# Modulation work ahead of the attention steps, gate rows by a product with ones, and one product less before the first unit

## Chip, cores and metric

One core of a Trainium2 chip runs the whole kernel; its time is the device time of one launch in microseconds (us). Engines are named as the profile names them: PE (TensorE matmul) and PEld (its weight load), DVE (VectorE), ACT (ScalarE), POOL (GpSimd), SP (SyncE, which here only starts transfers). Clock figures are the granted clock of PE, 1.00 being 2.4 GHz and 0.50 being 1.2 GHz.

## The reference

Two transformer blocks on one sequence of 256 tokens, width 2048, all in float32. What matters here is the first block's modulation: twelve thousand numbers computed from a condition vector c, in six parts of 2048 (shift, scale and gate of the two half-blocks).

```python
c_act = jax.nn.silu(c)
mod = c_act @ w_ada[l] + b_ada[l]                  # w_ada: 2048 x 12288
sh1, sc1, gt1, sh2, sc2, gt2 = [m[:, None, :] for m in jnp.split(mod, 6, axis=-1)]
h = rms_norm(x, g_norm1[l]) * (1 + sc1) + sh1
proj = h @ w_in[l]
...                                                # differential and latent attention, 8 heads each
mix = jnp.concatenate([a_out, b_out], axis=-1) @ w_out[l]
x = x + gt1 * mix
h2 = rms_norm(x, g_norm2[l]) * (1 + sc2) + sh2
ffn = (jax.nn.silu(h2 @ w_gate[l]) * (h2 @ w_up[l])) @ w_down[l]
x = x + gt2 * ffn
```

The second block (convolution and attention branches, a feed-forward of 8192) follows and is not touched.

## The kernel before

**Units.** All large products are made of units (`unit`, L620 on PE). A unit multiplies 256 rows of a weight matrix by 512 columns: 12 matmuls of 512 columns, since each float32 product is made as three products of float32r halves (high by high, high by low, low by high). A weight load is 1 MB and feeds two units. SP issues all loads in one fixed order (`ORDER`) into a ring of four buffers (`raw`); a load waits until the one four places before it is used up. Before a unit can run, ACT writes the high half of its weights (`split`, L1154), then DVE the low half (L1678). Each engine's program has one slot per unit: in its slot ACT and DVE make a split three units ahead, then do what hangs on that unit.

**Modulation.** w_ada comes in 96 loads `a`. The first 32 (`NPRO`) go through a ring of their own of four buffers (`early_mix`, `wide`), the rest through `raw`, between the weight loads. For loads 0 to 79 PE multiplies by the condition columns (`part_sums`, L643: four matmuls side by side, each with 32 output rows; 512 columns), and DVE copies or adds the bank into the tile `part` (L1724, L1729, L1731). When a group is complete, `part_columns` (L670) brings it to one number per partition: four small products with `sel` or `ones` (L677, L680), to which DVE adds the bias (L1747, L1759) in `mcol`. Loads 80 to 95 (gate gt2) are multiplied on DVE instead (`part_products`, L1697), inside the first loop of the feed-forward. The two gates gt1 and gt2 are needed as rows, the same in all partitions: `part_row` (L684, L690) multiplies each column of `mcol`, broadcast, by the identity, four matmuls of 128 columns for 512 numbers, and DVE copies the bank to `grow` (L1767), a tile that shares memory with `v_tok`.

**Where it is placed.** `prologue` (L110) lists the steps before the first unit: products 0 to 17, the turning of x (`normT`), the gains. `modulation(u)` (L127) lists the modulation steps of unit u: until unit 15 one product per unit, then a pair of products in each of 24 units between 24 and 98, with `columns` steps between them; gt1's groups are complete in units 88 and 100, and `gt1_row` makes its four rows behind units 93, 97, 101 and 105. gt2's groups get a column product in one unit of the loop and the row product in the next.

**Order within a slot.** On PE a unit's 12 matmuls come first, then `run(todo)`, the attention steps of this unit as listed by `window` and `heads_at`, and then `modulate()`:

```python
                last_mm.then_inc(unit_used, 1)
                run(todo)
                modulate()
```

DVE's slot has the same order: split, attention steps, modulation. ACT takes no part in the modulation but counts the banks. The small products of both kinds go through two PSUM banks in turn (`wait_bank`, L607): a step has to wait until the step two places before it has been read out, whoever reads it. Attention steps are, among others, `qbT`, `kvbT` (transposes, L716), `da` and `ha` (head products, L829, L855), `dc` (L838), with their DVE parts `qbN` (L2007), `kvbN` (L2031, L2034), `daW` and so on.

**First units.** ACT's order before the first unit is split 0, split 1, `modulated(0)` (L1273, scales the first chunks of x), split 2, `modulated(1)` and on; DVE's is column sums of the scale, split 0, split 1, its half of `modulated(0)` (L1931, L1932, which releases `h_ready`), split 2, `modulated(1)`.

## Time and profile before

| | us |
|---|---|
| median of 3 runs | 2669.9 (2666.29 to 2670.49) |
| profiled execution, its time | 2669.09 |
| its span in the profile | 2667.0 |
| PE busy | 2594.2 (97%) |
| DVE busy | 1547.3 (58%) |
| ACT busy | 1164.6 (44%) |
| PE's granted clock, mean | 0.989 |

The profiled execution's time is 0.8 us below the median of the runs and 2.1 us above its own span. PE is busy nearly all the time; the page's slices show lower values only in the first (6 tenths) and in those from 267 us to 600 us (down to 8 tenths). The transfers' share is 0.9 in the first two slices and 0.5 to 0.7 behind them. "Idle before" names, in brackets behind an instruction, how long its engine waited and who released it.

### The profile page before, as it was taken

How to read it: one execution, taken by the hardware profiler on the slowest of the kernel's cores; microseconds unless marked ns; L12 is line 12 of the kernel's file. 1: busy time of each engine (PE TensorE's matmuls, PEld its weight loads, DVE VectorE, ACT ScalarE, POOL GpSimd, SP SyncE). 2: the span in 40 equal slices, each digit the busy share in tenths (PEclk: the TensorE clock that was granted, in tenths of full speed). 3: DMA queues.
4: the chain of work that ended last, by engine and by line, in shares of the span. 5: the costliest groups of instructions: out<-in, count | busy, mean ns of one | idle time of the engine just before them, and what ended most of it. 6: DMA issues, size and time to landing. Idle time of an engine off the chain costs nothing.

```text
span 2667.0 us, 32922 instructions
## 1 busy us (share of the span) xinstructions
PE 2594.2 (97%) x12142; PEld 2084.7 (78%) x12142; DVE 1547.3 (58%) x1700; ACT 1164.6 (44%) x1522; POOL 53.9 (2%) x86
## 2 busy tenths in 40 slices
PE   6999989899999999999999999999999999999997
PEld 2667757688888888887888888888888888888886
DVE  1456754567776555557655454556555555555555
ACT  2344554343434444443544455444444444444443
POOL 1010110000000000000000000000000000000000
PEclk8999989999999999999999999999999999999999
DMA  9967776657777655555655545566565555555652
GB/s 391 381 232 288 261 252 220 223 171 244 243 244 245 192 190 189 189 190 189 206 189 189 174 158 166 196 201 226 188 200 189 190 188 189 189 189 188 190 188 100
DMA packets 262881, 561.72 MB, mean 211 GB/s; under 512 B 9250, under 2 KB 13556, under 8 KB 261900
## 3 DMA queue, kind: packets, MB, share of 16 engines
q1 hardware_dynamic: 260688, 549.25, 61.2%
q0 software_dynamic: 1728, 9.19, 1.0%
q10 hardware_dynamic: 380, 2.13, 0.2%
q8 instruction: 56, 0.92, 0.1%
q14 instruction: 29, 0.24, 0.0%
HBM read 556.32 MB, written 4.21 MB: 210 GB/s over the span
## 4 chain that ended last, share of the span: by engine, by line
PE 83%; DVE 2%; ACT 1%; issue 1%; DMA 0%; POOL 0%; DVEq 0%; POOLq 0%; ACTq 0%
PE acc L633 78%; PE bank L716 2%; PE bank L663 1%; DVE w_lo L1678 0%; PE acc L857 0%; PE acc L909 0%; PE acc L855 0%; PE bank L728 0%; PE bank L866 0%; DMA raw<-in_w_ada 0%; PE bank L690 0%; DVE wide L2194 0%; DVE x_res L2198 0%; PE acc L1068 0%; PE acc L1069 0%
## 5 line engine op out<-in xcount | busy, mean ns | idle before, releaser
L1678 DVE TENSOR_TENSOR w_lo<-raw,w_hi 128x1024 fp32r<-128x1024 f32 x852 | 1037.7, 1224 | 827.5 <-ACT w_hi L1154 798.6
L1154 ACT ACTIVATE w_hi<-raw 128x1024 fp32r<-128x1024 f32 x852 | 901.0, 1060 | 1065.1 <-PE acc L633 953.8
L633 PE MATMUL acc<-w_hi,actT_hi 128*128 128x512 f32 (+1 forms) x2112 | 833.6, 395 | 1.2 <-DVE actT_lo L1813 0.8
L633 PE MATMUL acc<-w_hi,actT_lo 128*128 128x512 f32 (+1 forms) x2112 | 821.2, 389 | 0.0
L633 PE MATMUL acc<-w_lo,actT_hi 128*128 128x512 f32 (+1 forms) x2112 | 820.8, 389 | 0.0
L633 PE MATMUL acc<-w_hi,mixT_hi 128*128 128x512 f32 (+1 forms) x1280 | 504.3, 394 | 9.1 <-DVE mixT_lo L1803 4.3
L633 PE MATMUL acc<-w_hi,mixT_lo 128*128 128x512 f32 (+1 forms) x1280 | 498.0, 389 | 0.0
L633 PE MATMUL acc<-w_lo,mixT_hi 128*128 128x512 f32 (+1 forms) x1280 | 497.6, 389 | 0.0
L633 PEld LDWEIGHTS acc<-w_hi,actT_hi 128*128 128x128 f32 x2112 | 397.3, 188 | 106.5 <-issue 21.9
L633 PEld LDWEIGHTS acc<-w_hi,actT_lo 128*128 128x128 f32 x2112 | 397.1, 188 | 83.0
L633 PEld LDWEIGHTS acc<-w_lo,actT_hi 128*128 128x128 f32 x2112 | 397.7, 188 | 79.3 <-issue 1.2
L633 PEld LDWEIGHTS acc<-w_hi,mixT_hi 128*128 128x128 f32 x1280 | 241.1, 188 | 67.5 <-issue 9.4
L633 PEld LDWEIGHTS acc<-w_hi,mixT_lo 128*128 128x128 f32 x1280 | 240.9, 188 | 49.7
L633 PEld LDWEIGHTS acc<-w_lo,mixT_hi 128*128 128x128 f32 x1280 | 241.3, 189 | 47.5
L2171 DVE TENSOR_TENSOR x_res<-x_res,acc 128x1024 f32<-128x1024 f32 x68 | 83.0, 1221 | 30.4 <-PE acc L633 30.4
L663 PE MATMUL bank<-raw,ccol 128*32 128x512 f32 x384 | 48.8, 617 | 5.4 <-DMA raw<-in_w_ada 3.1
L716 PE MATMUL bank<-cst,work 128*128 128x128 f32 x356 | 47.9, 274 | 5.5 <-DVE att L2034 2.5
L716 PEld LDWEIGHTS bank<-cst,work 128*128 128x128 f32 x356 | 41.8, 141 | 13.9 <-DVE att L2034 2.9
L2171 DVE TENSOR_TENSOR wide<-wide,acc 128x1024 f32<-128x1024 f32 x36 | 44.0, 1221 | 14.5 <-PE acc L633 14.5
L1202 ACT ACTIVATE mixT_hi<-bank 128x512 fp32r<-128x512 f32 (+1 forms) x54 | 25.6, 503 | 60.6 <-PE bank L716 37.4
L1458 ACT ACTIVATE work<-acc,kpe 128x512 f32<-128x512 f32 x48 | 30.4, 686 | 39.3 <-PE acc L633 39.3
L1707 DVE SCALAR_TENSOR_TENSOR part<-raw,ccol,part 128x512 f32<-128x512 f32 x60 | 45.1, 751 | 1.7
(272 smaller groups left out, 1049.1 us busy)
## 6 DMA issues: line engine op xcount, KB each, us to landing
raw<-in_w_ff SPq DMA_DIRECT2D x128, 1024.0 KB, 5.1
raw<-in_w_in SPq DMA_DIRECT2D x108, 1024.0 KB, 5.2
raw<-in_w_ada SPq DMA_DIRECT2D x64, 1024.0 KB, 5.2
raw<-in_w_gate SPq DMA_DIRECT2D x44, 1024.0 KB, 5.1
raw<-in_w_up SPq DMA_DIRECT2D x44, 1024.0 KB, 5.2
raw<-in_w_down SPq DMA_DIRECT2D x44, 1024.0 KB, 5.1
early_mix<-in_w_ada SPq DMA_DIRECT2D x16, 1024.0 KB, 9.5
wide<-in_w_ada SPq DMA_DIRECT2D x16, 1024.0 KB, 8.8
```

The source lines that it names most:

```text
L633: last_mm = pe.matmul(acc[p][:, t, 0:width], act[x][:, k0 + c, t * P:(t + 1) * P], w[:, u % SPL, c * NW:c * NW + width], start=first and c ...
L663: ins = pe.matmul(dst[32 * j:32 * j + 32, :], ccol[:, 2 * r + j // 2 if n_ == 8 else 4 * r + j, :], src[:, j * NW:(j + 1) * NW], start=beg ...
L716: ins = pe.transpose(bank[b][:, j * P:(j + 1) * P], src_of(j), ident)
L1154: act.activation(w_hi[:, u % SPL, :], raw[:, ld % RAW, (u % DU) * 1024:(u % DU + 1) * 1024], ACT.Copy) \
L1202: act.activation(dst, bank[b][:, 0:n], ACT.Copy).then_inc(bank_hi, 1)
L1458: ins = act.activation(stg[:, t * NW:(t + 1) * NW], acc[p][:, t, :], ff, scale=scale[:, t:t + 1])
L1678: dve.tensor_tensor(w_lo[:, u % SPL, :], raw[:, ld % RAW, (u % DU) * 1024:(u % DU + 1) * 1024], w_hi[:, u % SPL, :].bitcast(F32), ALU.subt ...
L1707: ins = dve.scalar_tensor_tensor(out=part[:, :], in0=src, scalar=ccol[:, k, 0:1], in1=part[:, :], op0=ALU.mult, op1=ALU.add)
L2171: link(dve.tensor_tensor(dst[:, :, g * NW:(g + 1) * NW], dst[:, :, g * NW:(g + 1) * NW], acc[g % 2][:, :, :], ALU.add))
```

## The change

1. **Order in a slot.** On PE, DVE and in ACT's count of banks, the modulation steps of a unit come ahead of its attention steps.
2. **Gate rows.** The `columns` step of the six groups of gt1 and gt2 goes, and with it `gt1_row`. In its place `part_row` multiplies `part` itself: two matmuls of 512 columns with a broadcast column of `sel` for a group of gt1 (1024 numbers), two of 256 columns with `ones` for one of gt2 (512 numbers), each in a bank of its own. DVE no longer copies but adds the bank to `grow`, which holds the bias already: POOL loads it, spread over all partitions (1 MB), gt1's behind the last differential head, gt2's once x is updated. gt1's rows are now made in units 88 and 100. gt2's column and row steps are now one step, in the unit of the former column step.
3. **First unit.** Product 17 moves from the prologue into unit 0, behind its matmuls. On DVE split 0 comes ahead of the last `columns` step of the prologue, split 1 behind `modulated(0)`.
4. The bias rows of gt1 and gt2 are no longer loaded at the start (two small transfers of POOL less).

```diff
-    return steps + [("part", LEAD), ("part", LEAD + 1)]
+    return steps + [("part", LEAD)]
...
-        return [LEAD + 1 + v] if 0 < v < NPRO - LEAD - 1 else []
-    events = [("row", n) for a in products(u - 3) for n in completed(a) if n >= len(GROUPS)]
-    events += [("columns", n) for a in products(u - 2) for n in completed(a)]
+        return [LEAD + 1 + v] if 0 <= v < NPRO - LEAD - 1 else []
+    events = [("row" if n >= len(PROLOGUE) + 4 else "columns", n) for a in products(u - 2) for n in completed(a)]
...
                 last_mm.then_inc(unit_used, 1)
+                modulate()
                 run(todo)
-                modulate()
...
-            def part_row(n_, kind=GT2, g=0):
-                pe.wait_ge(mod_ready, L.value("groups", n_ + 1))
-                b, _ = wait_bank()
-                for j in range(4):
-                    col = mcol[:, kind, 4 * g + j:4 * g + j + 1]
-                    ins = pe.matmul(bank[b][:, j * P:(j + 1) * P], col.broadcast_to([P, P]), ident, start=True,
-                                    stop=True)
-                ins.then_inc(bank_full[b], 1)
+            def part_row(n_):
+                pe.wait_ge(part_ready, L.value("groups", sums_of(n_), 4))
+                for j in range(2):
+                    b, _ = wait_bank()
+                    if n_ < len(GROUPS):
+                        pe.matmul(bank[b][:, :], sel[:, j:j + 1].broadcast_to([P, P]), part[:, :], start=True,
+                                  stop=True).then_inc(bank_full[b], 1)
+                    else:
+                        pe.matmul(bank[b][:, 0:S], ones[:, :], part[:, j * S:(j + 1) * S], start=True,
+                                  stop=True).then_inc(bank_full[b], 1)
...
             pool.wait_ge(lgt_full, H)
             pool.wait_ge(o_ready, H)
+            pool.dma_start(grow, b_ada("gt1").partition_broadcast(P)).then_inc(gt1_bias, 16)
...
             inv_rms(D, TT)
+            pool.wait_ge(xg_ready, 4)
+            pool.dma_start(grow, b_ada("gt2").partition_broadcast(P)).then_inc(gt2_bias, 16)
...
+            def part_row(n_):
+                for j in range(2):
+                    b = next_bank()
+                    if n_ < len(GROUPS):
+                        dve.wait_ge(gt1_bias, 16)
+                        at_ = (2 * (n_ - len(PROLOGUE) - 4) + j) * NW
+                        dst, sums = grow[:, at_:at_ + NW], bank[b][:, :]
                     else:
+                        dve.wait_ge(gt2_bias, 16)
+                        dst, sums = grow[:, bass.ds(j * S if L.i is None else L.i * NW + j * S, S)], bank[b][:, 0:S]
+                    link(dve.tensor_tensor(dst, sums, dst, ALU.add))
                     dve.sem_inc(bank_free[b], 1)
...
             for s in prologue():
+                if s == ("columns", 1):
+                    split()
                 if s[0] in todo_of:
                     todo_of[s[0]](*s[1:])
-            for _ in range(DU):
-                split()
             modulated(0)
-            for _ in range(AHEAD - DU):
+            for _ in range(AHEAD - 1):
                 split()
```

## Rows read from the trace of the kernel before

**Rows 1.** Stretches: us, busy PE, PEld, DVE, ACT, POOL (count), PEclk, DMA, GB/s.

```profile
66.00:133.00 67.00, 66.83 (x348) 43.20 (x347) 28.79 (x39) 24.21 (x29) 1.00 (x1) 1.00 1.01 383
...
325.00:389.00 64.00, 50.43 (x255) 35.92 (x248) 37.07 (x81) 32.77 (x109) 10.82 (x18) 0.87 0.66 228
```

**Rows 2.** Timeline, first units: start, us, instruction, idle before and its releaser.

```profile
59.29 0.69 DVE L1932 TENSOR_TENSOR actT_lo<-xT,actT_hi 128x512 fp32r<-128x512 f32 x1
...
59.93 1.94 PE L663 MATMUL bank<-early_mix,ccol 128*32 128x512 f32 x8 [0.85 <-DMA early_mix<-in_w_ada]
...
62.38 1.06 ACT L1154 ACTIVATE w_hi<-raw 128x1024 fp32r<-128x1024 f32 x1 [4.79 <-DMA raw<-in_w_in]
...
65.07 0.69 DVE L1932 TENSOR_TENSOR actT_lo<-xT,actT_hi 128x512 fp32r<-128x512 f32 x1
...
65.81 0.19 PEld L633 LDWEIGHTS acc<-w_hi,actT_hi 128*128 128x128 f32 x1 [0.44 <-DVE actT_lo L1932]
```

**Rows 3.** Timeline, one gt2 group: column product, row product, the units behind them.

```profile
612.03 0.95 PE L680 MATMUL bank<-ones,part 128*128 128x1 f32 x8
...
613.16 0.39 PE L633 MATMUL acc<-w_lo,actT_hi 128*128 128x512 f32 x1
...
615.69 1.05 PE L690 MATMUL bank<-cst,mcol 128*128 128x128 f32 x8
...
616.82 0.39 PE L633 MATMUL acc<-w_lo,actT_hi 128*128 128x512 f32 x1
```

**Rows 4.** Timeline: two long fp32 products, each behind a bare unit.

```profile
140.61 1.02 PE L780 MATMUL bank<-wide,att 128*128 128x512 f32 x2
...
144.24 1.02 PE L780 MATMUL bank<-wide,att 128*128 128x512 f32 x2
```

**Rows 5.** Waits of the PE, 325 to 389 us: total, times, longest.

```profile
PE bank L716 <- DVEq L1735: 3.0, 1, 3.0
...
PE acc L855 <- DVEq L1785: 2.2, 1, 2.2
...
PE bank L677 <- ACT k_nope L1196: 1.4, 1, 1.4
```

**Rows 6.** Stretch 325 to 349 us, columns as in the first group.

```profile
325.00:349.00 24.00, 18.56 (x116) 14.89 (x109) 21.21 (x45) 13.36 (x40) 2.62 (x4) 0.93 0.70 244
```

**Rows 7.** Timeline of the attention stretch, 333 to 389 us.

```profile
333.47 0.68 DVE L1731 TENSOR_TENSOR part<-part,bank 128x512 f32<-128x512 f32 x1
...
366.51 1.23 DVE L1678 TENSOR_TENSOR w_lo<-raw,w_hi 128x1024 fp32r<-128x1024 f32 x1 [0.78 <-ACT w_hi L1154]
...
368.85 0.79 PE L909 MATMUL acc<-w_hi,mixT_hi 128*128 128x512 f32 x1 [0.27 <-DVEq L1785]
...
374.14 0.79 PE L716 MATMUL bank<-cst,work 128*128 128x128 f32 x4
...
379.90 0.68 DVE L2031 TENSOR_TENSOR work<-acc,rstd 128x512 f32<-128x512 f32 x1
...
381.19 1.89 PE L855 MATMUL acc<-k_nope,q_nope 128*128 128x256 f32 x4 [2.18 <-DVEq L1785]
...
385.01 3.47 PE L663 MATMUL bank<-raw,ccol 128*32 128x512 f32 x16
```

**Rows 8.** Timeline, unit 30: head product, and the modulation product that waits.

```profile
182.85 1.05 PE L838 MATMUL bank<-v_tok,att 128*128 128x128 f32 x8
...
185.06 1.06 PE L663 MATMUL bank<-raw,ccol 128*32 128x512 f32 x8 [0.16 <-DMA raw<-in_w_ada]
```

**Rows 9.** Waits of the PE, 133 to 325 us, that its modulation products have.

```profile
PE bank L663 <- DMA raw<-in_w_ada: 2.3, 4, 1.1
...
PE bank L663 <- DVE mixT_lo L1803: 0.6, 1, 0.6
```

**Rows 10.** Short stretches behind idle time, columns as in the first group.

```profile
334.00:336.00 2.00, 1.74 (x6) 1.74 (x7) 1.37 (x2) 2.00 (x9) 0.00 (x0) 0.50 0.39 55
...
368.00:370.00 2.00, 1.73 (x6) 1.45 (x7) 1.07 (x5) 0.00 (x0) 0.00 (x0) 0.50 0.45 81
```

More of the change, by code:

```diff
@@ L44 @@
                                ("sh2", 16))),
-                      (ROWS2, (("sc2", 16), ("gt1", 16), ("gt2", 16), ("gmix", 16), ("gmlp", 16), ("convw", 24),
+                      (ROWS2, (("sc2", 16), ("gmix", 16), ("gmlp", 16), ("convw", 24),
                                ("gq", 1), ("gk", 1), ("gqn", 1), ("gkn", 1)))):
@@ L151, in banks_of @@
 def banks_of(u):
-    return len([1 for e in modulation(u) if takes_bank(*e)])
+    return sum(2 if what == "row" else 1 for what, n_ in modulation(u) if takes_bank(what, n_))
 def pieces_of(n_):
@@ L927, in _ @@
             for g in range(4):
-                at = {1: lambda g=g: gt1_row(g)}
-                if g == 0:
-                    at = {0: lambda: run(heads_at(16)), 1: lambda: [run(heads_at(17)), gt1_row(0)],
-                          2: lambda: run(heads_at(18))}
+                at = {j: lambda j=j: run(heads_at(16 + j)) for j in range(3)} if g == 0 else None
                 group(g % 2, MIXT, 8, k0=8, at=at, ready=(lambda j: outputs_taken(H + UC * j)) if g == 0 else None)
@@ L1166, in unit @@
                 L.next("unit")
+                skip_banks(banks_of(L.n["unit"] - 1))
                 run(todo)
-                skip_banks(banks_of(L.n["unit"] - 1))
             def units(n, at=None):
@@ L1410, in _ @@
                 if g == 0:
-                    at = {0: lambda: run(heads_at(16)), 1: lambda: [run(heads_at(17)), skip_banks(1)],
-                          2: lambda: run(heads_at(18))}
+                    at = {j: lambda j=j: run(heads_at(16 + j)) for j in range(3)}
                 else:
-                    at = {0: lambda g=g: group_sums(g - 1), 1: lambda: skip_banks(1)}
+                    at = {0: lambda g=g: group_sums(g - 1)}
                 units(4, at)
@@ L1612, in _ @@
             b_ada = lambda name: A["b_ada"][0, PARTS.index(name) * D:(PARTS.index(name) + 1) * D]
-            for name, src in (("sc2", b_ada("sc2")), ("gt1", b_ada("gt1")), ("gt2", b_ada("gt2")),
-                              ("gmix", A["g_mix_2"][0, :]), ("gmlp", A["g_mlp_2"][0, :]),
+            for name, src in (("sc2", b_ada("sc2")), ("gmix", A["g_mix_2"][0, :]), ("gmlp", A["g_mlp_2"][0, :]),
                               ("convw", A["conv_w_2"][0, :, :].rearrange("j n -> (j n)"))):
@@ L1739, in part_columns @@
                 b = next_bank()
[L1740 to L1751 removed]
+                kind, k0, width = GROUPS[n_]
@@ new lines, in part_columns @@
+                name = PARTS[kind]
+                cols, rows_ = (cols1, ROWS1) if name in ROWS1 else (cols2, ROWS2)
+                at_ = lambda base: slice(base + k0, base + k0 + width)
+                dst, sums, bias = mcol[:, kind, at_(0)], bank[b][:, 0:width], cols[:, at_(rows_[name][0])]
+                if width == 8:
+                    link(dve.tensor_tensor(dst.rearrange("p (h j) -> p h j", h=2),
+                                           sums.rearrange("p (j h) -> p h j", h=2),
+                                           bias.rearrange("p (h j) -> p h j", h=2), ALU.add))
+                else:
+                    link(dve.tensor_tensor(dst, sums, bias, ALU.add))
@@ L1752, in part_columns @@
                     dve.sem_inc(bank_free[b], 1)
-                    if name in ("sc1", "sc2"):
-                        link(dve.scalar_tensor_tensor(out=dst, in0=dst, scalar=1.0,
-                                                      in1=cols1[:, at_(ROWS1["g" + name[2]][0])], op0=ALU.add,
-                                                      op1=ALU.mult))
-                else:
-                    at_ = ROWS2["gt2"][0] + 4 * (n_ - len(GROUPS))
-                    link(dve.tensor_tensor(mcol[:, GT2, 0:4], bank[b][:, 0:4],
-                                           cols2[:, at_:at_ + 4] if L.i is None else cols2[:, bass.ds(L.i * 4 + at_, 4)],
-                                           ALU.add))
-                    dve.sem_inc(bank_free[b], 1)
@@ L2129, in _ @@
             for g in range(4):
-                at = {1: lambda g=g: gt1_row(g)}
-                if g == 0:
-                    at = {0: lambda: run(heads_at(16)), 1: lambda: [run(heads_at(17)), gt1_row(0)],
-                          2: lambda: run(heads_at(18))}
-                units(4, at)
+                units(4, {j: lambda j=j: run(heads_at(16 + j)) for j in range(3)} if g == 0 else None)
                 if g == 0:
```

32 lines of the change are left out of this document (10 added, 22 removed).

## The prediction

> **What bounds it now.** I first read the stretches, to see where PE is not at work. From 66 to 133 us it is busy for 66.83 of 67.00 us [rows 1], and where gt2 is made, in the loop of the feed-forward, its products stand between units with no idle time [rows 3]: there any product taken from PE's queue shortens the kernel, and nothing else does. From 325 to 389 us it is busy for only 50.4 of 64 us, and its mean clock is 0.87 [rows 1]. This stretch holds the last heads of the differential attention and the turn to the latent one. Then I read PE's waits in it: the longest are for a bank that DVE frees after a modulation addition (3.0 us), for an accumulator that DVE frees (2.2 us), and a `columns` step that waits for ACT (1.4 us) [rows 5]. Next I asked which engine is full while PE waits: from 325 to 349 us DVE is busy for 21.2 of 24 us [rows 6]. Last the timeline of the first units, since part of the change is there [rows 2]. Everything behind 822 us is untouched.
>
> **Gate rows.** Matmuls of a unit start 0.23 us apart ((615.69 - 613.16)/11), so a bare unit takes 2.76 us [rows 3]. A column product starts at 612.03 and the unit's second matmul at 613.16: 1.13 less 0.23 is 0.90 us. A row product, from 615.69 to 616.82, costs the same 0.90 [rows 3]. What comes in is a float32 product with 128 output rows and 512 columns. The trace has one of this very shape, the mirror product: two of them stand 3.63 us apart with one unit between, so one costs 0.87 us [rows 4].
> - gt1: two column products and four row products, 6 x 0.90 = 5.4 us, become four products of 512 columns, 4 x 0.87 = 3.5. Gain 1.9 us. They stand where PE goes from unit to unit without a wait.
> - gt2: in each of four turns 0.90 + 0.90 becomes two products of 256 columns. Together they stream as many columns as one of 512, so I take 0.90; no row shows one of 256, and the bounds are 0.87 (nothing but columns) and 1.74 (each as dear as one of 512). Gain 4 x 0.90 = 3.6 us, at least 0.2.
>
> Together 5.5 us, between 2.1 and 5.6. DVE's work stays nearly the same: an addition out of a bank takes 0.68 us [rows 7], and it replaces a copy of the same size. That DVE now waits in its slot for two products instead of one delays its next split, which is three units ahead of PE (8 us); the cover is there. The two new loads go through POOL's queue. gt1's comes ahead of the small bias load and the reload of x, which PE's work needs some 90 us later; gt2's falls where PE waits for the normalisation. At full share the stretch would move 228/0.66 = 345 GB/s [rows 1], so 1 MB is 3 us of transfer time; without the cover each would cost up to that, and with it I cost them at nothing. DVE would stall in unit 88 if the bias were not there: its load is released at about 383 us and the unit is 60 us later. The two loads dropped at the start release nobody: 0.
>
> **First unit.** Product 17 waits 0.85 us for its load, starts at 59.93 and keeps unit 0 back until 61.9 (59.93 + 1.94); the first chunk of x is ready at 59.98 (59.29 + 0.69) [rows 2]. So unit 0 could start 1.9 us sooner, and DVE's new order doesn't spoil it: split 0 needs ACT's half and takes about as long ahead of the column sums as it took behind them, while split 1, no longer ahead of `modulated(0)`, gives that time back. But what is late next? Unit 1 starts at 65.82, and the row says why: it waited for the second chunk of x (65.07 + 0.69) [rows 2]. In front of this chunk ACT has split 2, which waited 4.79 us for a weight load that landed at 62.38 [rows 2], and the change leaves ACT's order as it is. Unit 0 started sooner takes the same 4 us at the low clock, product 17 comes behind it, and unit 1 still begins at 65.8. I take 0; the bounds are a gain of 1.9 us (the whole of product 17) and a loss of 0.5. Product 17 ends later, so its buffer is refilled up to 3.6 us later; the transfers behind it stay queued (share 1.01 [rows 1]) and PE had no wait there.
>
> **The new order, place by place.** Every pair of products moved ahead of attention steps makes PE do 1.9 us of sure work first, and DVE do its addition (0.68 us) and wait for PE before its own attention steps.
> - Unit 30: the products' second load lands at 185.06 and PE waited for it even behind 1.0 us of head product (182.85 to 183.84) [rows 8]. With the cover gone: 1.0 us lost. Of the three others of these four waits (2.3 us in all, the longest 1.1 [rows 9]), two have a transpose of 0.3 us in front: 0.6 lost.
> - The longest, 1.1 us, is unit 56's [rows 9], with nothing in front. Its load is issued once DVE has added the pair of unit 54, and this addition comes 2 us sooner in the new order: 1.1 gained. The wait of 0.6 us for a bank [rows 9], in unit 64, and a like one in unit 24 go too: 1.0 gained. So far +0.5 us.
> - 325 to 349 us: the wait of 3.0 us was for a bank whose reader, the addition at 333.47, stood in DVE's queue behind a normalisation and a head [rows 5, 7]. It goes. But DVE is full here, and PE next needs the accumulator and the split that come out of the same queue, in which the addition now stands in front: I take 0.7 us lost (one addition), with bounds of 3.0 gained and, below, a loss.
> - Units 74 and 75: the wait of 1.4 us of the `columns` step goes [rows 5], but unit 75 starts at 368.85, when DVE has freed its accumulator, and DVE came to this from its split at 366.51, which had waited for ACT [rows 7]. The column additions (0.6 us with their links) now stand between: 0.65 lost.
> - Unit 76: its matmuls end at 379.0, PE waits 2.2 us for the accumulator of the head product, does this at half clock until 385.01, and then the pair takes 3.47 us, until 388.5 [rows 7]: 9.5 us. In the new order the pair fills the wait (1.9 us at full clock, to 380.9); DVE adds (0.7) and normalises (1.3, from 379.90 to 381.19 [rows 7]), to 382.9; the head product takes 1.9 us at full or 3.8 at half clock, to 384.8 or 386.7. Gain 3.7 or 1.8; I take 2.8.
> - From 389 to 530 us PE hardly waits, and order alone moves nothing.
>
> Sum: 0.5 - 0.7 - 0.65 + 2.8 = 2 us gained (1.95), between 8.6 gained and 3 lost.
>
> **Sum.** 5.5 + 0 + 2 = 7.5 us, so the profiled execution would take 2669.1 - 7.5 = 2661.6. It stands 0.8 us below the median, so the predicted median is 2662.4, 0.28% less.
>
> **The clock.** Behind the wait of 3.0 us the granted clock is 0.50 from 334 to 336 us, and behind the waits of units 74 and 75 again from 368 us [rows 10]; there a unit takes 5.3 us (368.85 to 374.14) instead of 2.76 [rows 7, 3]. In the new order the wait at 331 doesn't vanish, it joins the one for the accumulator behind the next unit, in one gap of about 5 us, so the unit behind it may run at 1.2 GHz. The Trainium skill (TensorE: Matmul & The Clock Gate, "Why this matters for your kernels") asks for no long idle gaps between bursts of matmuls, since the clock falls behind them; by this rule the change gives 2.5 us back at this place, and the trace agrees that gaps are followed by the low level.
>
> **Rivals.**
> - *The clock takes it back.* One more unit at 1.2 GHz costs 5.3 - 2.76 = 2.5 us [rows 7, 3], and unit 76 gains only 1.8: 2669.9 - 5.5 - 0.5 + 0.7 + 0.65 - 1.8 + 2.5 = 2666.0. For it: the joined gap. Against it: DVE is behind anyway, so a slower PE may hide in its lag.
> - *All waits vanish.* DVE catches up, and the 3.0, 1.4 and 3.7 us are gained in full, with 0.5 besides: 2669.9 - 5.5 - 8.6 = 2655.8. For it: the waits named in the rows are for banks and not for data. Against it: 21.2 of 24 us.
> - *The first unit counts in full.* Unit 1's chunk comes as much sooner: 1.9 us more, 2660.5 [rows 2]. Against it stands the row with the landing at 62.38.
> - *PE is not freed by the rows.* The products of 256 columns cost as much as long ones, or waits for their banks take the rest: gain 2.1 + 2, 2665.8.
> - *Slower: DVE is made to wait.* In the slots of units 66, 70, 72 and 76 DVE must wait for PE's pair and add it (1.9 + 0.68 = 2.6 us) before the normalisations that PE waits for next. If none of this is hidden, that is 4 x 2.6 = 10.4, and with the slow unit 12.9 us, against 5.5 of the rows: 2677.3. It decides the sign once three of the four delays reach PE. Against it: DVE had come to these slots late, so PE's pair is mostly done when DVE asks for it.
>
> **Chances.** Forecast (2662.4, itself 2659 to 2665) 0.47; clock 0.17; all waits 0.10; first unit 0.07; rows not freed 0.10; slower 0.09. About 0.2%, 5.3 us, is what a measurement of this kernel tells from no change. Faster by more (below 2664.6): 0.42 of the forecast, 0.10, 0.07 and 0.03 of the others, 0.62. Slower by more (above 2675.2): 0.07. The rest, 0.31, is the same. The range of 8 in 10 takes in the clock, the unfreed rows and the first unit and reaches to the low outer rival: 2656 to 2670.
>
> **What the profile after would show.** Right: two products of 512 columns with about 0.87 us each in units 88 and 100; in the loop one stop of about 0.9 us per turn instead of two; unit 0 near 60 us and unit 1 still near 65.8; PE's wait at L716 for a modulation bank gone and a wait for an accumulator of 4 to 5 us in its place; the pair of unit 76 ahead of its head product, with the end of both at about 385 to 387 less what was gained before; the wait for load `a` in unit 30 about 1 us. Wrong: unit 1 well before 65; DVE idle for PE's pairs in slots 66 to 76; a wait of DVE for a gate's bias; PE's time between 390 and 530 us longer by more than 1 us apart from the rows.

## The result, and the profile after

The changed kernel takes 2673.4 us (median of 16 runs, 2671.5 to 2675.4), the kernel before 2668.8 us (16 runs beside it, 2665.3 to 2672.9). The ratio is 1.0018, with a 95% interval of 1.0011 to 1.0025: 4.7 us slower. The forecast was 2662.4 us, 0.28% faster than before. The profiled execution of the changed kernel took 2673.26 us, its span is 2670.9 us.

The head of its page (busy us, share of the span, instructions):

```profile
span 2670.9 us, 32740 instructions
PE 2590.6 (97%) x12054; PEld 2076.6 (78%) x12054; DVE 1546.9 (58%) x1698; ACT 1167.4 (44%) x1522; POOL 54.5 (2%) x86
```

PE is busy for 3.6 us less than before (2594.2) while the span is 3.9 us longer, so PE is idle for 7.5 us more. The stretches say where. They answer to [rows 1] and [rows 6]; columns as there.

```profile
66.00:133.00 67.00, 67.00 (x350) 43.41 (x348) 28.91 (x39) 23.88 (x28) 1.00 (x1) 1.00 1.00 382
325.00:389.00 64.00, 48.45 (x252) 35.06 (x248) 34.81 (x74) 32.51 (x107) 9.13 (x16) 0.84 0.56 201
325.00:349.00 24.00, 16.88 (x84) 13.13 (x84) 16.19 (x35) 12.27 (x39) 3.43 (x6) 0.79 0.64 227
```

From 325 to 349 us PE does 1.7 us less than before, and DVE, which was full (21.2 us of 24), now works for 16.2 us: it waits too. PE's waits from 325 to 400 us (what was waited for: us in total, times, longest), to be read against [rows 5]:

```profile
PE bank L715 <- ACT q_nope L1192: 3.3, 1, 3.3
PE bank L664 <- DMA raw<-in_w_ada: 2.9, 1, 2.9
PE acc L908 <- DVEq L1780: 2.5, 2, 1.3
PE bank L715 <- DVEq L1748: 2.3, 1, 2.3
PE acc L854 <- DVEq L1780: 2.2, 1, 2.2
```

(Lines: L715 is L716 of before, L664 is L663, L908 is L909, L854 is L855, L1780 is L1785.) The wait of 3.0 us for the modulation bank is gone, and in its place stand one of 3.3 us for ACT's copy `q_nope` and one of 2.9 us for a load `a`. The wait for the accumulator ahead of the head product of unit 76 is 2.2 us, exactly what it was, though the pair now stands in front of it.

The two traces can be laid on each other unit by unit, since PE signals the end of every unit. The table gives how much later (+) or sooner a unit ends in the changed kernel than in the one before, at a few units, worked out from these signals (of units 72 to 75, which work in pairs, only the second of a pair signals, once for each of its halves):

| end of unit | before, us | changed kernel | what lies between |
|---|---|---|---|
| 0 | 65.82 | -1.95 | product 17 moved |
| 1 | 68.84 | -0.44 | |
| 24 | 159.35 | -1.15 | 0.71 in unit 18, also in kernels with the old prologue |
| 64 | 314.80 | +1.05 | pairs of units 24 to 60 |
| 71 | 348.61 | +6.33 | pairs of units 64 to 70 |
| 76 | 379.02 | +8.63 | slots of units 72 and 74 |
| 77 | 391.46 | +6.92 | pair and head product of unit 76 |
| 107 | 522.01 | +6.60 | pairs; gt1's rows |
| 221 | 865.38 | +0.87 | unit 108 with the normalisation ahead of it -1.9; gt2's rows 4 x -0.96 |
| 365 | 1266.04 | +3.74 | one wait at 1258 us, and the clock behind it |
| 851, the last | 2654.45 | +3.89 | |

### The profile page after: what moved, and what is told of

The parts are those of the page before. It is cut to its first block, busy times and chain, and to the rows that moved or that the text cites. A ratio compares the mean times of both kernels' runs of the same rounds, so it can differ in the third digit from the quotient of the medians.

```text
span 2670.9 us, 32740 instructions
## 1 busy us (share of the span) xinstructions
PE 2590.6 (97%) x12054; PEld 2076.6 (78%) x12054; DVE 1546.9 (58%) x1698; ACT 1167.4 (44%) x1522; POOL 54.5 (2%) x86
## 4 chain that ended last, share of the span: by engine, by line
PE 91%; DVE 3%; DMA 3%; ACT 1%; issue 1%; POOL 0%; DVEq 0%; SPq 0%; POOLq 0%; ACTq 0%
PE acc L634 83%; PE bank L715 2%; PE bank L664 2%; DMA raw<-in_w_ada 1%; DMA early_mix<-in_w_ada 1%; DVE w_lo L1675 1%; DMA raw<-in_w_in 0%; PE acc L856 0%; PE acc L908 0%; PE bank L727 0%; PE bank L865 0%; ACT w_hi L1150 0%; PE acc L854 0%; PE acc L664 0%; ACT probs L1358 0%
## 5 line engine op out<-in xcount | busy, mean ns | idle before, releaser
L664 PE MATMUL bank<-raw,ccol 128*32 128x512 f32 x384 | 48.1, 607 | 8.4 <-DMA raw<-in_w_ada 8.3
L715 PEld LDWEIGHTS bank<-cst,work 128*128 128x128 f32 x356 | 41.8, 142 | 17.7 <-issue 6.0
L715 PE MATMUL bank<-cst,work 128*128 128x128 f32 x356 | 48.9, 277 | 5.8 <-DVE att L2029 1.7
L1597 POOL TENSOR_SCALAR rstd<-ss 128x2 f32<-128x2 f32 (+2 forms) x27 | 6.8, 253 | 1949.9 <-DVE ss L1828 1709.9
```

What stands on the lines that cost most here:

```text
L664: ins = pe.matmul(dst[32 * j:32 * j + 32, :], ccol[:, 2 * r + j // 2 if n_ == 8 else 4 * r + j, :], src[:, j * NW:(j + 1) * NW], start=beg ...
L715: ins = pe.transpose(bank[b][:, j * P:(j + 1) * P], src_of(j), ident)
L1597: link(pool.tensor_scalar(slot, ss[:, 0:n], 1.0 / width, EPS, ALU.mult, ALU.add))
```

## The experiments

Each median is set against the runs of the kernel before in the same series (2667.6 to 2668.5 us). A difference to before has an uncertainty of about 2.5 us (intervals of 0.09% on either side; of 0.13% or 3.6 us for `order_only` and `half_old`, which have 5 runs each), one between two experiments of about 3.5, so a step of a single place rests on the traces. "Old order" is attention steps first, "new order" modulation first.

### Three parts, one by one

`order_only`: before, and on PE, DVE and in ACT's count of banks

```
-                run(todo)
                 modulate()
+                run(todo)
```

> The kernel before with only the order within a slot changed: on PE, DVE and in ACT's count of banks the modulation steps come ahead of the attention steps. Gate rows and prologue are as before. Theory 1 (the order is what costs): set side by side by the ends of units, the two traces drift apart by +2.2 us between units 30 and 60 and by +7.7 us between units 66 and 76, and get 1.7 us back in unit 77; so about +8 us against the kernel before, 2675 to 2680. Theory 2 (the loads of the gate biases, 1 MB each, are what costs; the order gives what the prediction said): about -2 us, 2665 to 2668. Theory 3 (nothing but the granted clock, which falls at other places): within 2 us of the kernel before.

`rows_only`: before with the new `part_row` and POOL's two loads of the bias.

> The kernel before with only the gate rows changed: part_row by two products, DVE adds to the bias that POOL has loaded; attention steps first as before, prologue as before. Theory 1: the four turns of the loop give 0.96 us each and gt1's rows some 1.9 us, so -5.7 us, 2662 to 2664.5. Theory 2: the two loads of 1 MB push weight loads back and take the gain away, -1 to +3 us, 2668 to 2672. Theory 3: -5.5 us as predicted, like theory 1.

`first_only`: before with

```
-    return steps + [("part", LEAD), ("part", LEAD + 1)]
+    return steps + [("part", LEAD)]
...
+                if s == ("columns", 1):
+                    split()
```

> The kernel before with only the first unit changed: product 17 behind unit 0, and DVE's splits 0 and 1 in their new places. From the trace of the changed kernel unit 0 ends 1.95 us sooner, unit 1 only 0.44 us, and unit 18 1.15 us sooner. All theories of the order and of the rows agree here: -0.4 to -1.2 us, about 2668; a gain of 1.9 us would say that unit 1 didn't hold it back.

`rows_first`: the changed kernel with the old order in all slots.

> The changed kernel with the old order in every slot (attention steps first), so the gate rows and the first unit of the change together. Theory 1: the sum of both, -6.5 us, 2661.5 to 2663.5, the fastest of the four, and 11 us below the changed kernel. Theory 2: 2667 to 2671. Theory 3: about 2663, but the kernel with the order alone is then no slower than before.

| kernel | median, us | against before | ratio, 95% |
|---|---|---|---|
| order_only | 2678.0 | +9.4 | 1.0038 (1.0024 to 1.0051) |
| rows_only | 2663.1 | -5.4 | 0.9979 (0.9970 to 0.9988) |
| first_only | 2668.6 | 0.0 | 1.0001 (0.9992 to 1.0010) |
| rows_first | 2664.0 | -4.6 | 0.9984 (0.9975 to 0.9993) |

The three parts add up to +4.0, the whole change measured +4.7. So the order costs what the change loses, the gate rows give what was forecast, and the first unit gives nothing that the medians can show. By the ends of unit 24 it gives a little: this unit ends at 159.1 us on average in the four profiles with the old prologue and at 158.5 in the thirteen with the new one (`x_sooner` left aside). `rows_first` was expected at -6.5 and measured -4.6. Theory 1 stands; the loads of the bias (theory 2) take nothing away, and DVE never waits for them.

### Which slots

Two causes are set against each other from here on. Theory A: pairs that move forward lose the work that covered their loads, so PE waits for loads. Theory E: DVE and ACT wait for PE's pair in their slots, and PE then waits for them. (Theory B is the prediction; C and D put the loss down to the clock of one execution.)

The changed kernel, with the new order on PE, DVE and in ACT's count of banks only where a condition on the unit holds, here for `order_64_75`:

```
+def modulation_first(L):
+    u = L.n["unit"] - 1
+    return 64 <= u < 76
```

> The changed kernel with the new order only in the units below 64 and the old order from there on. The base to compare with is the changed kernel with the old order everywhere, 2664.0 us. Theory A (the loads of the pairs lose their cover): the unit ends of the order-only kernel drift by 1 to 1.5 us here, in the units behind 30, 36, 40 and 46, where PE waits for load a, so 2665 to 2666. Theory B (the steps of the prediction): +1.0 +0.6 -1.1 -1.0, that is -0.5 us, 2663.5.

> The changed kernel with the new order only in units 64 to 75, the old order elsewhere; base 2664.0 us. Theory A: unit 66's pair now waits 2.9 us for its second load, PE falls to the low clock and the queue of DVE and ACT behind it is entered later; with unit 70 and the 1.07 us each behind units 71 and 73 this makes +5 to +7 us, 2669 to 2671. Theory B (prediction): 0.7 + 0.65 = +1.35 us, 2665.3. Theory C (the drift was the clock of one execution): within 1 us of the base.

> The changed kernel with the new order only from unit 76 on, the old order before; base 2664.0 us. Theory B (prediction): unit 76's pair fills the wait for the accumulator, -2.8 us, 2661.2. Theory D (the 9.5 us of the old order in unit 76 were the low clock of the one execution that was profiled; three other kernels with the same code there take 3.3 us less): nothing is left to gain, and with 0.19 us in each of four pairs behind it the kernel is 0 to 2.5 us slower than the base, 2664 to 2666.5.

> The changed kernel with the new order in unit 66 only, the old order elsewhere; base 2664.0 us. Theory A (load waits): the second load of this pair is waited for 2.9 us and PE falls to the low clock, so most of the 4.0 us of units 64 to 75 are here, 2667 to 2668. Theory E: about +1.5 us here, since the wait of 3 us for a bank behind unit 68 takes part of the delay up, 2665 to 2666.

> The changed kernel with the new order in units 70, 72 and 74 only; base 2664.0 us. No load is waited for here. Theory E: 1.07 us each behind units 71 and 73, where DVE now adds before it frees the accumulator, and up to 1 us in unit 70: +2 to +3 us, 2666 to 2667. Theory A: 0 to +0.7 us.

| new order in units | median, us | against before | against rows_first (-4.6) |
|---|---|---|---|
| below 64 | 2666.5 | -1.6 | +2.9 |
| 64 to 75 | 2668.0 | -0.2 | +4.4 |
| 76 and on | 2665.4 | -2.7 | +1.8 |
| 66 alone | 2666.2 | -2.1 | +2.5 |
| 70, 72, 74 | 2664.7 | -3.5 | +1.0 |
| all (the change) | 2673.4 | +4.7 | +9.2 |

The first three add up to +9.1 us of 9.2. By the medians only the stretch from 64 to 75 is clear of its error of 3.5 us. None is seen to gain, not even the one from unit 76 on, which carried the forecast. The last two rows are too close to their errors to share out 4.4 us.

The ends of units in all profiles can. The table has how long PE takes from the end of one unit to that of another, in the profiles with the new order there and in those without (loads at full length). A profile is one execution, but each row has several on both sides:

| from unit to unit | old order there, us | new order there, us | means differ by |
|---|---|---|---|
| 24 to 64 | 155.4 to 156.7 (11 profiles) | 157.3 to 158.8 (4) | 1.8 |
| 64 to 71 | 33.3 to 35.8 (11) | 37.5 to 39.1 (5, new in unit 66) | 3.8 |
| 71 to 76 | 29.6 to 30.7 (10) | 32.3 to 32.7 (6, new in units 72 and 74) | 2.5 |
| 77 to 107, with the new gate rows | 129.1 to 129.2 (8) | 130.2 to 130.4 (3) | 1.2 |

So of units 64 to 75 the slot of unit 66 costs the most. `order_66` alone takes 37.65 us from 64 to 71. The pair of unit 70 costs nothing: `order_70_74` and `cover_kept`, which have the new order there and the old one in unit 66, take 33.33 and 34.16 us and stand among the old ones. In the fourth row `new_dve_late_76` is left out; it has 131.59 us, with a wait of 1.2 us for the load of unit 80 that the others don't have.

### Load waits, or engines that wait for each other

In the stretch below unit 64 most of it is the loads. PE's waits from 133 to 325 us, first of `rows_first`, then of `order_24_63` (L674 is the product of a pair, L725 a transpose):

```profile
PE bank L674 <- DMA raw<-in_w_ada: 3.2, 4, 1.1
```

```profile
PE bank L674 <- DMA raw<-in_w_ada: 5.5, 4, 1.6
PE bank L725 <- DVEq L1754: 0.7, 2, 0.4
```

2.3 us more for the same four loads; between the ends of units 24 and 64 this kernel takes 158.78 instead of 156.32 us, 2.5 more. That is the largest such difference; the mean is 1.8. The changed kernel has 4.0 us of these load waits. With short loads (below) the new order still takes 1.0 us more here (154.56 against 153.56), so the loads are not all of it.

For the stretch behind, `half_new` and `half_old` (new and old order in every slot) load only half of each `a` from 32 to 79. They leave out the other half of the operand: PE multiplies what the buffer held, and what these modulation numbers feed is not the reference's. Instructions and waits stay as they are.

```
-                    load(view, i, per, width=width, kind="a")
+                    load(view[:, 0:1, :], i, per, width=width, kind="a")
```

> The changed kernel, but of each of the loads a 32 to 79 of w_ada only the first half (512 KB instead of 1 MB) is loaded; the other half of the operand is what the buffer held, so shift, scale and gate 1 of the second half-block are not the reference's. Order, waits and instructions are unchanged, only these transfers are short. To be read against the same kernel in the old order (half_old). Theory A (the pairs lose the cover of their loads): without load waits the difference between the two orders falls from 9.5 us to about 4. Theory E (DVE and ACT are made to wait for PE's pairs): the difference stays at 8 to 10 us.

> The same short loads a 32 to 79 (only half of the data of each) in the changed kernel with the old order in every slot. PE waits there for such loads 2.3 us between 133 and 325 us and 1.5 us in unit 98, so about 3 to 4 us below its counterpart with whole loads (2664.0): 2660 to 2661. Its difference to half_new tells theory A (about 4 us) from theory E (8 to 10 us).

Measured: 2668.3 and 2657.6 us, a difference of 10.6 us (known to some 4), where theory A expected 4. PE's waits in `half_new` from 322 to 352 us, where the changed kernel waited 2.9 us for a load:

```profile
PE bank L715 <- ACT q_nope L1192: 3.9, 1, 3.9
PE acc L634 <- DVEq L1780: 2.2, 2, 1.2
```

The load wait is gone, and the wait for `q_nope` is 3.9 us instead of 3.3. From the end of unit 64 to that of unit 76 the new order takes 70.42 us with short loads and the old 64.15, 6.3 us apart; with whole loads it is 71.80 and 65.64 (`rows_first`), 6.2 apart. With the loads out of the way the new order costs as much, so theory A falls here: a load wait in unit 66 only stands in front of a wait that would come anyway. `order_76_on`, with the old order in unit 66, shows the same from the other side. It waits there for its loads from 322 to 352 us,

```profile
PE bank L674 <- DMA raw<-in_w_ada: 2.0, 2, 1.8
```

and unit 67 ends 3.7 us later against the one before than in the kernel before. But then the wait of 3.0 us for the modulation bank does not come, and from 64 to 71 it takes 33.99 us like the others.

> The changed kernel with the old order in four units only, 30, 40, 46 and 66, the ones whose second load is issued late and waited for. Theory A: 1 to 1.5 us come back in the first three and 3 to 4.4 us in unit 66, so 2668 to 2670 instead of 2673.4. Theory E: only what PE's own pair costs is saved, 2672 to 2673.5.

`cover_kept` has the old order in units 30, 40, 46 and 66 and the new one elsewhere. Measured: 2668.2 us, +0.6 against before where the change had +4.7, so 4.0 us back. That is what theory A expected, but it doesn't speak for the loads: the old order in unit 66 also puts DVE's and ACT's work there back, and the short loads show that this is what counts.

Then the direct test of theory E, in unit 76. PE does its pair first, DVE keeps the old order (in this slot DVE's attention steps use no bank, so the count of banks still agrees). `pe_first_76` has the old order in all other slots, `new_dve_late_76` the new one:

```
 # unit() of DVE, in pe_first_76
+                first = False
...
 # unit() of DVE, in new_dve_late_76
+                first = L.n["unit"] - 1 != 76
+                if not first:
+                    run(todo)
```

> The changed kernel with the old order in every slot, except that in unit 76 PE alone does its pair ahead of the head product; DVE there still normalises first and copies the bank behind it. Base: the old order everywhere, 2664.0 us. Theory E (in the new order DVE waits for PE's pair before it normalises, and PE waits for the normalisation): now the pair fills PE's wait of 2.2 us for the accumulator, unit 77 ends 1.9 us sooner, 2661.5 to 2662.5. If something else sets the end of the wait: 2664.

> The changed kernel, new order everywhere, but DVE in unit 76 alone normalises before it waits for the pair. Theory E: PE's wait of 2.2 us for the accumulator behind the pair goes nearly whole, so about 2 us less than the changed kernel, 2671 to 2672. If the wait has another cause: 2673.4.

What happens in unit 76 of the changed kernel, PE's rows and then DVE's (start, us, instruction, idle before):

```profile
387.57 1.92 PE L664 MATMUL bank<-raw,ccol 128*32 128x512 f32 x16
391.69 0.45 PE L854 MATMUL acc<-k_nope,q_nope 128*128 128x256 f32 x1 [2.20 <-DVEq L1780]
...
389.56 0.69 DVE L1726 COPY part<-bank 128x512 f32<-128x512 f32 x1 [0.96 <-PE bank L664]
390.40 0.69 DVE L2026 TENSOR_TENSOR work<-acc,rstd 128x512 f32<-128x512 f32 x1
```

DVE is idle for 0.96 us until PE's pair is done, copies its bank, and only then normalises; PE waits for that. The pair doesn't fill PE's wait, it pushes it 1.9 us back. In `pe_first_76` (L674, L864, L1748, L1802 and L2048 are L664, L854, L1726, L1780 and L2026 of the changed kernel):

```profile
379.44 1.92 PE L674 MATMUL bank<-raw,ccol 128*32 128x512 f32 x16
381.68 0.45 PE L864 MATMUL acc<-k_nope,q_nope 128*128 128x256 f32 x1 [0.32 <-DVEq L1802]
...
380.39 0.68 DVE L2048 TENSOR_TENSOR work<-acc,rstd 128x512 f32<-128x512 f32 x1
...
384.68 0.68 DVE L1748 COPY part<-bank 128x512 f32<-128x512 f32 x1
```

Now DVE normalises while PE does the pair, and PE's wait is 0.32 us. From the end of unit 76 to that of unit 77 this kernel takes 7.28 us; with the old order on both engines, in executions without a fall of the clock there, it is 9.15. Medians: 2660.0 us for `pe_first_76` (ratio to before 0.9971, 0.9960 to 0.9982; the fastest of the kernels that load everything) and 2672.0 for `new_dve_late_76`, where PE's wait is 0.3 us as well (+3.7 against before where the change had +4.7; too close for the medians, but its trace has the same 7.28 us, but it takes 1.4 us more again behind unit 80, where PE waits for a load). `pe_first_76` gains 3.7 us on `rows_first` and not only the 1.9 of the wait. One possible reason is the clock: neither of the two profiles has a fall in unit 76, while 4 of 11 in the old order have. That is not shown.

The same pattern stands in units 72 and 74. Unit 72 of the changed kernel:

```profile
360.99 0.68 DVE L1728 TENSOR_TENSOR part<-part,bank 128x512 f32<-128x512 f32 x1
...
361.79 0.33 PE L715 MATMUL bank<-cst,att 128*128 128x128 f32 x1 [0.76 <-DVEq L1732]
...
362.32 0.56 DVE L2002 TENSOR_TENSOR work<-acc,rstd 128x384 f32<-128x384 f32 x1 [0.65 <-PE bank L715]
...
363.46 0.50 PE L908 MATMUL acc<-w_hi,mixT_hi 128*128 128x512 f32 x1 [1.23 <-DVEq L1780]
```

The addition stands ahead of the normalisation that frees PE's accumulator: PE's transpose waits 0.8 us for the bank that the addition frees, DVE's normalisation 0.65 us for the transposes, and PE 1.2 us for the accumulator ahead of unit 73. Before, PE waited 1.2 us ahead of the pair (for ACT's `q_nope`) and for neither of these. From the end of unit 71 to the first signal of unit 73 it takes 1.07 us more than in `rows_first`. Slot 74 costs 1.06 us in the same way, and the traces of `order_70_74` (+1.06 and +1.03) and `order_64_75` (+1.07 and +1.04) have both again. `order_70_74` was expected at 2 to 3 us above `rows_first`; its median has +1.0, its trace these 2.1.

In units 66 to 70 the chain is longer. The changed kernel (DVE, ACT, and PE's wait at its end):

```profile
337.89 1.22 DVE L2052 TENSOR_REDUCE nmx<-probs 128x4 f32<-128x1024 f32 x1
...
339.14 0.51 ACT L1358 ACTIVATE probs<-probs,nmx 128x256 f32<-128x256 f32 x1 [3.01 <-DVE nmx L2052]
...
342.07 0.67 ACT L1192 ACTIVATE q_nope<-bank,cols 128x512 f32<-128x512 f32 x1
...
342.89 0.45 PE L715 MATMUL bank<-cst,att 128*128 128x128 f32 x1 [3.32 <-ACT q_nope L1192]
```

ACT's copy of the bank stands behind the softmax of a differential head (four exponentials) and a split, and the softmax behind DVE's normalisation, head and maximum. In the old order PE waited 3.0 us for the modulation bank while ACT worked this off; in the new order PE runs one more unit and then waits 3.3 us for the same chain. The wait has moved by a unit and has not become shorter. The traces of `order_66` and `order_64_75` show this too: unit 69 ends 3.4 us sooner against the one before than in `rows_first`, unit 70 then 4.0 and 3.6 us later.

Waits are not all that the new order adds. From the end of unit 64 to that of unit 76 the changed kernel takes 71.8 us where the kernel before took 64.2, 7.6 more. PE's waits in it grow from 11.9 to 16.2 us, 4.3. The other 3.3 us are the same instructions done slower: the granted clock is 0.50 for 20.5 us of this stretch, before for 10.2. All profiles with the new order in unit 66 have 0.50 for 6.8 us or more between units 64 and 71, all others for 3.4.

### The first unit

`x_sooner`: the second scaling of x ahead of split 2 on ACT and DVE, in `rows_first`. On DVE:

```
             modulated(0)
-            for _ in range(AHEAD - 1):
+            split()
+            modulated(1)
+            for _ in range(AHEAD - 2):
                 split()
...
```

> The changed kernel with the old order in every slot, and besides the second scaling of x ahead of split 2 on ACT and on DVE, so that the second chunk of x doesn't stand behind the weight load which lands at 62 us. The prediction says that this chunk is what holds unit 1: then unit 1 ends 1 to 1.9 us sooner and the kernel takes 2662 to 2663 us (base 2664.0). If something else holds it (the low clock, unit 2's split), it is the same as the base within 0.5 us.

Measured: 2663.8 us, -3.8 against before, like `rows_first` (-4.6), so the scaling sooner gains nothing that shows. The wait of PE for the second chunk (0.53 us in the changed kernel) is gone: the chunk is ready at 61.6 us. But unit 0 itself runs at the low clock,

```profile
60.00:62.00 2.00, 2.00 (x6) 1.60 (x5) 1.53 (x3) 0.00 (x0) 0.00 (x0) 0.50 1.05 398
```

product 17 follows it, and unit 1 starts at 65.17 where the changed kernel has 65.38. It ends 0.5 us sooner than in `rows_first`, and by the end of unit 18 these 0.5 us are gone, 0.26 of them in a wait for the load of `bias_by_distance` that `rows_first` doesn't have.

### The kernel before once more

> The kernel before once more, unchanged, for a second look at its clock. Theory D: the granted clock falls at other places than in the first execution, so that unit 77 ends some 3 us sooner against the first profile, and the stretch about 1260 us, which took no clock fall in the first profile, may take one (1.6 to 2.9 us). If the falls belong to the program: the ends of all units agree with the first profile within 0.3 us.

It took 2671.15 us in its one run. The fall at 381 us came again (unit 76 to 77: 12.41 us, the first profile 12.44), that at 334 us didn't; it came at 346 us, and units 65 to 71 took 2.0 us longer. So some of the falls move from one execution to the next. From the end of unit 76 to that of unit 77, with the old order, 11 profiles show 9.0 to 9.2 us seven times and 12.4 us four times. `rows_first` (first) has the waits of the kernel before, and the high clock where `before_again` (second) has the low one:

```profile
384.00:386.00 2.00, 2.00 (x16) 0.79 (x18) 0.86 (x2) 0.21 (x1) 2.00 (x4) 1.00 1.10 424
386.00:388.00 2.00, 2.00 (x14) 1.16 (x7) 0.90 (x2) 1.76 (x5) 0.07 (x1) 1.00 1.01 412
```

```profile
384.00:386.00 2.00, 2.00 (x5) 1.17 (x4) 0.00 (x0) 0.00 (x0) 1.93 (x3) 0.50 0.95 356
386.00:388.00 2.00, 2.00 (x8) 0.87 (x10) 0.41 (x1) 0.00 (x0) 0.39 (x1) 0.50 0.99 221
```

## Why the prediction was wrong, step by step

What failed is the sum of the new order: forecast 2 us gained, measured 9.2 to 9.4 us lost. The gate rows came as forecast, so the sign of the whole change hung on it. By the ends of units the five terms of that sum came to 1.8, 3.8, 2.5, 0 and 1.2 us lost, 9.3 in all, where 0.5 gained, 0.7 lost, 0.65 lost, 2.8 gained and 0 were forecast. The two largest errors, some 3 us each, are the attention slots of units 66 to 71 and unit 76.

**Gate rows: right.** Forecast -5.5, measured -5.4 (`rows_only`). In each turn of the loop, where two products of 256 columns with `ones` stand between units,

```profile
616.51 0.40 PE L634 MATMUL acc<-w_hi,actT_lo 128*128 128x512 f32 x1
616.74 1.03 PE L694 MATMUL bank<-part,ones 128*128 128x256 f32 x4
617.42 0.58 PE L634 MATMUL acc<-w_hi,actT_hi 128*128 128x512 f32 x1
```

the old kernel lost 1.80 us and this one 0.84, so 0.96 is gained (0.90 was forecast), four times. gt1 gave 1.5 us by the ends of units 88 and 107 in `rows_only`, where 1.9 was forecast. The two products per slot cost what was said (unit 89, behind the slot of unit 88, ends 0.82 later), but one of the four row products taken away let PE come sooner to unit 98's second load, and it waits 0.8 us more there; with the short loads this place is 1.0 us shorter. "They stand where PE goes from unit to unit without a wait" was not true of that one.

**First unit: right.** Forecast 0, measured 0.0 (`first_only`), or 0.6 gained by the ends of unit 24, both inside its bounds. The wait for the second chunk is in the trace as expected, but it wasn't all: with it removed the low clock in unit 0 is next.

**Units 24 to 64: the step "so far +0.5 us" gained fails.** The new order loses 1.8 us here (2.9 by the median of `order_24_63`, 2.5 by its trace). The 1.0 us of unit 30 was about right: its load wait is 0.38 us in `rows_first`, 1.27 in `order_24_63` and 1.35 in the changed kernel. For units 40 and 46 the 0.6 was right in size but not steady: 0.65 and 0.70 us in `order_24_63`, 0.15 and 0.04 in the changed kernel. What failed are the gains. Of the 1.1 us booked for unit 56 the changed kernel has half (the wait is 0.55 us where `rows_first` has 1.14) and `order_24_63` nothing (1.23), and where it shrank, a wait of 0.41 us for DVE stood behind it in unit 59. Of the 1.0 us booked for the banks in units 24 and 64 some 0.2 came: waits of 0.43 and 0.63 us gave way to others of 0.28 and 0.58. And unit 35 got a new wait of 0.4 for the bank that DVE's addition frees.

**325 to 349 us: the step "0.7 us lost" is mis-sized; the runs show 3.8 us from unit 64 to 71.** The wait of 3.0 us went, as said, and the joined wait came. But the prediction looked for what is late next on DVE alone. ACT's copy of the bank, which stands behind the softmax, was next (3.3 us). And unit 66, whose second load had 1.6 us of attention work as cover (322.9 to 324.5 us in the kernel before), was not in the list of places. PE waits 2.9 us there, and the clock is at 0.50 behind it. This wait is not the cause of the loss, though, since it stays without it; the chain through ACT and the clock behind it are.

**Units 72 to 75: right in kind, mis-sized.** Forecast 0.65 lost, measured 1.07 in slot 72 and 1.06 in slot 74, and 2.5 from unit 71 to 76. Only 74 was counted; in 72 the addition stands in front of an accumulator as well.

**Unit 76: the largest gain in the sum.** Forecast 2.8 gained. The new course was forecast well: its sum lets PE's head product start 3.9 us behind the end of the unit (382.9 against 379.0), and it starts 4.0 behind it (391.69 against 387.65); the unit after it starts 6.4 us behind, where 5.8 or 7.7 were forecast. So the chain "pair, DVE adds, DVE normalises" stood in the sum, with a wait of 2.0 us behind the pair (380.9 to 382.9), as long as the one that the pair was said to fill (2.2). What failed is the price of the old order: the 9.5 us [rows 7] contained some 3.3 us that only the low clock explains (12.4 against 9.15 from unit end to unit end), and 7 of 11 profiles of the same code don't have them. At full clock the forecast's own terms give 2.2 + 1.9 + 1.9 = 6.0 us for the old order and 5.8 for the new: no gain but 0.2. Measured without the falls the place takes 9.15 us in the old order and, taking some 1.7 us off its 10.73 for the 3.4 us in which the clock is at 0.50, about 9.0 in the changed kernel. Against the one profile of before the place did gain 1.71 us, close to the 1.8 of the forecast's slow case; that is the luck of which execution was profiled. The gain was there to have, with DVE left in its old order (7.28 us).

**389 to 530 us: "order alone moves nothing" fails by 1.1 us.** It is 0.19 us in each of four pairs, and 0.3 behind unit 88. That is just over the 1 us that the prediction had named as a sign of being wrong. The other sign that came is DVE idle for PE's pairs in these slots (1.57 us in unit 66, 0.96 in unit 76).

**The rivals.** The one that came nearest is "DVE is made to wait": it had slots 66, 70, 72 and 76 and 10.4 us, and the order cost 9.4 us. Its mechanism is what the traces show in slots 66, 72, 74 and 76. That its number is so near is luck: it put 2.6 us on each slot, while unit 70 costs nothing, unit 76 nothing without a fall, and 3 us of the loss come from places that it doesn't name (below unit 64 and behind 77). It was dismissed because "DVE had come to these slots late", which was carried over from one place and not read slot by slot.

"The clock takes it back" came in part, at the place where it was looked for. The joined gap is there: between unit 69 and unit 70 PE does two transposes in 4.9 us (339.57 to 344.48). The unit behind it runs at the low clock,

```profile
344.00:346.00 2.00, 1.52 (x5) 1.52 (x6) 1.69 (x7) 2.00 (x10) 0.64 (x2) 0.50 0.65 119
```

as the section of the Trainium skill (TensorE: Matmul & The Clock Gate, "Why this matters for your kernels") would have it. The clock is less than half of what the order costs in these slots (3.3 us of 7.6 between the two profiles, units 64 to 76), and the waits are the rest.

Two more pieces of the difference between the two profiles belong to no part of the change. At 1258 us PE waits 3.3 us in both kernels. Behind it, before (first) kept the high clock and the changed kernel (second) didn't:

```profile
1260.00:1262.00 2.00, 1.69 (x7) 1.42 (x8) 1.34 (x2) 0.00 (x0) 0.00 (x0) 1.00 0.00 0
1262.00:1264.00 2.00, 2.00 (x10) 1.67 (x9) 0.00 (x0) 0.60 (x1) 0.00 (x0) 1.00 0.69 174
```

```profile
1262.00:1264.00 2.00, 2.00 (x6) 1.52 (x6) 0.21 (x1) 0.00 (x0) 0.00 (x0) 0.50 0.28 48
1264.00:1266.00 2.00, 2.00 (x6) 1.52 (x5) 0.00 (x0) 0.00 (x0) 0.00 (x0) 0.50 1.03 373
```

This is 2.9 us between the two traces. Of 18 profiles of this and its sister kernels, 6 have no fall there, 9 a whole one (2.5 us and more) and 3 a part.

The other is the -1.9 us at unit 108 in the table of unit ends. Ahead of this unit PE waits 7.4 or 7.5 us and then 0.8 us in both kernels, for the normalisation; the mean clock over the place is 0.60 before (first) and 0.77 in the changed kernel (second):

```profile
522.00:539.00 17.00, 8.78 (x30) 7.47 (x31) 7.76 (x12) 4.32 (x9) 0.90 (x2) 0.60 0.21 65
```

```profile
528.60:543.70 15.10, 6.78 (x30) 5.99 (x31) 7.86 (x12) 4.33 (x9) 1.50 (x3) 0.77 0.34 133
```

8 of the 18 profiles take 15.1 us here and 10 take 16.6 to 17.4, with the old and the new order in both groups. Between the two profiles that are compared the two pieces come to +1.0 us.

What stays open: how much of the loss in unit 66 is the wait that moved and how much the clock behind it, since every profile with the one has the other; and whether the new order makes falls of the clock more likely in unit 76. All five profiles with the new order on both engines there have at least part of one, four of the eleven with the old.

## What to carry to other kernels

When work A is moved ahead of work B on an engine that waits, it must be asked of every engine that shares the slot whether it now waits for A before it does the B that the first one needs. In unit 76 moving it on PE alone filled the wait (1.9 us); moving it on both engines left the wait whole. A wait for a buffer is often parallel to a longer chain on a third engine (here DVE, ACT, bank): removing it moves the wait to the chain's end. And a duration that contains a fall of the clock, read from one execution, is no price; it is compared with a second profile, or with the same code in another kernel, before it goes into a sum.

## What the runs showed of the hardware

A low-clock stretch behind a wait of 2 to 3.3 us is not a property of the program alone: the same wait of 3.3 us is followed by 1.00 in 6 and by 0.50 in 9 of 18 executions (in 3 for a part of the time), and costs 0 or some 2.5 us. Behind the wait of 2.2 us in unit 76 it is 0 or 3.3 us (7 and 4 of 11 executions), and at unit 108 the time differs by 2 us in the same way. By an estimate from these three, all falls together make some 8 us, as much as the runs of one kernel spread (2665 to 2673 us); that they make the spread is not shown. A float32 product of 256 columns between units costs half of one of 512: 0.42 us (0.84 for two) against 0.86 (1.72 for the pair in unit 88, from 0.82 and the 0.90 of the column product that it replaces), so here it goes by columns alone.
